# The feed-forward networks of a two-layer trunk: up products first, then the down product as seven accumulated block products

## The reference

```python
def conv_ffn(h, w_up, conv_w, conv_b, w_down):
    a = h @ w_up                                  # 256x1024 @ 1024x5632
    a = lax.conv_general_dilated(a, conv_w[:, None, :], window_strides=(1,), padding=((1, 1),),
                                 feature_group_count=2 * D_FF, ...) + conv_b
    g, u = jnp.split(a, 2, axis=-1)
    return (jax.nn.gelu(g, approximate=True) * u) @ w_down    # 256x2816 @ 2816x1024

# in each of two layers:
    h = rms_norm(x, ffn_pre_g[l])
    x = x + rms_norm(conv_ffn(h, ...), ffn_post_g[l])
```

## Time and profile before

| what | us |
|---|---|
| time, median of 3 runs (1779.08 to 1784.57) | 1782.12 |
| span of the profiled execution, first to last instruction | 1778.3 |
| TensorE busy | 1723.2 |
| VectorE busy | 812.8 |
| ScalarE busy | 412.3 |
| GpSimd busy | 76.2 |

### The profile page before, as it was taken

How to read it: one execution, slowest core, us unless ns; L and a number is a source line. 1 busy time by engine, 2 the same in 40 slices (tenths; PEclk the granted TensorE clock), 3 DMA queues, 4 the chain that set the end, 5 groups by cost and what they waited for, 6 DMA issues and landing times.

```text
span 1778.3 us, 28776 instructions
## 1 busy us (share of the span) xinstructions
PE 1723.2 (97%) x11902; PEld 1392.8 (78%) x11902; DVE 812.8 (46%) x1807; ACT 412.3 (23%) x903; POOL 76.2 (4%) x68
## 2 busy tenths in 40 slices
PE   7999999999999999999999999999999899999997
PEld 4767787666656666679788889999897688899996
DVE  4898444111111111145534445665566344576665
ACT  3743311000000000021632221111314522311112
POOL 1012001000000000010002110000000010000000
PEclk9999999999999999999999999999999999999999
DMA  9121784999999999954323244444443133244420
GB/s 396 76 71 63 294 329 178 396 422 422 422 422 422 422 421 422 422 217 144 117 95 142 95 142 157 156 165 163 146 148 139 63 127 119 95 166 166 161 77 24
DMA packets 53662, 383.50 MB, mean 216 GB/s; under 512 B 6080, under 2 KB 6336, under 8 KB 7360
## 3 DMA queue, kind: packets, MB, share of 16 engines
q1 hardware_dynamic: 52272, 376.91, 54.1%
q10 hardware_dynamic: 1296, 5.24, 0.8%
HBM read 381.08 MB, written 1.05 MB: 215 GB/s over the span
## 4 chain that ended last, share of the span: by engine, by line
PE 91%; DVE 5%; ACT 2%; DMA 1%; POOL 1%; issue 1%; POOLq 0%; ACTq 0%; DVEq 0%
PE ps L630 88%; PE ps L628 2%; DVE arena L2199 2%; PE ps L687 1%; DVE arena L2205 1%; DMA xT<-in_xc 1%; POOL arena L523 1%; DVE small L2770 0%; ACT arena L1985 0%; DVE arena L2615 0%; DVE arena L2202 0%; ACT arena L2058 0%; ACT arena L1747 0%; DVE xT L2199 0%; DVE small L2199 0%
## 5 line engine op out<-in xcount | busy, mean ns | idle before, releaser
L630 PE MATMUL ps<-arena,ring 128*128 128x256 f32 (+2 forms) x3248 | 602.5, 343 | 9.6 <-DVE arena L2199 2.1
L630 PEld LDWEIGHTS ps<-arena,ring 128*128 128x128 f32 x3248 | 507.4, 191 | 83.4 <-issue 37.6
L630 PE MATMUL ps<-ring,arena 128*64 128x256 f32 (+5 forms) x3120 | 458.1, 414 | 0.0
L630 PE MATMUL ps<-arena 128*128 128x128 f32 (+6 forms) x3178 | 416.3, 292 | 4.9 <-ACT arena L2058 1.7
L630 PEld LDWEIGHTS ps<-arena 128*128 128x128 f32 (+3 forms) x3178 | 381.9, 190 | 29.4 <-issue 14.1
L630 PEld LDWEIGHTS ps<-ring,arena 128*64 128x64 f32 (+1 forms) x3120 | 272.9, 147 | 168.1 <-issue 84.4
L2199 DVE TENSOR_TENSOR arena<-arena,ps 128x256 f32<-128x256 f32 (+2 forms) x256 | 98.5, 404 | 208.9 <-ACT arena L1955 202.8
L2205 DVE SCALAR_TENSOR_TENSOR arena<-arena,par 128x255 f32<-128x255 f32 (+1 forms) x282 | 125.7, 488 | 6.5 <-ACT arena L2175 2.3
L630 PE MATMUL ps<-ring 128*128 128x256 f32 (+2 forms) x896 | 114.4, 291 | 0.4 <-issue 0.4
L2670 DVE COPY arena<-ps 128x128 f32<-128x128 f32 x60 | 17.5, 291 | 207.4 <-PE ps L630 207.4
L630 PEld LDWEIGHTS ps<-ring 128*128 128x128 f32 (+2 forms) x896 | 97.2, 154 | 13.6 <-issue 1.9
(11 more groups left out here) (197 smaller groups left out, 1031.6 us busy)
## 6 DMA issues: line engine op xcount, KB each, us to landing
ring<-in_stream SPq DMA_DIRECT2D x358, 1024.0 KB, 9.9
arena<-in_xc ACTq DMA_DIRECT2D x1, 1024.0 KB, 6.2
xT<-in_xc ACTq DMA_DIRECT2D x1, 1024.0 KB, 10.7
arena<-in_mem ACTq DMA_DIRECT2D x1, 1024.0 KB, 4.7
out_y<-xT ACTq DMA_DIRECT2D x2, 512.0 KB, 2.6
ring<-in_dft ACTq DMA_DIRECT2D x1, 512.0 KB, 8.7
arena<-in_sguw ACTq DMA_DIRECT2D x2, 256.0 KB, 3.0
row<-in_row SPq DMA_DIRECT2D x1, 474.0 KB, 24.3
```

Source lines behind the costliest of these rows:

```text
L630: i = nc.tensor.matmul(out, lhsT, rhs, start=start, stop=stop, skip_group_check=skip)
```

## The change

The plain down slots become block products too, and the order changes. Nothing else of the computation is touched; three semaphores are folded into others, and a DMA scratch area is made smaller to give room to a tensor `extra`.

- The up slots of all pairs come first, then the eleven down slots. The stream of weights is stored in that order. All eleven gated products are kept (`f_all`).
- `down(steps)`: seven block products for each of four groups p of output chunks (banks 2p and 2p + 1), 28 products with 128 moving columns in a slot, accumulated over all slots in PSUM in all eight banks, joined once at the end (four joins into `ffn_out`). The first down slot takes the groups in the order 2, 3, 0, 1, since banks 0 to 3 still hold the last up slots; the last two slots are done together, group by group.
- `slot_sums(n)`, VectorE: weight sums of slot n, three slots ahead of TensorE (three buffers `wf` in place of two); for a down slot (n >= 20) also four sums of blocks of the gated product, on 128x128.
- VectorE per pair: join w = 0, slot sums, join w = 1, slot sums, side taps, gated product.
- `y_squares` reads the joined result instead of PSUM.

```diff
-                up_first()
-                for i in range(FFN_PAIRS):
-                    if i + 1 < FFN_PAIRS:
-                        up(i + 1)
-                    down(i)
+                up_first()
+                for i in range(1, FFN_PAIRS):
+                    up(i)
+                for i in range(FFN_PAIRS - 2):
+                    down([i])
+                down([FFN_PAIRS - 2, FFN_PAIRS - 1])
+                pe.wait_ge(cb_ok, joins_at(l, "down", 1))
...
-                def down(i):
-                    s = arrive()
-                    pe.wait_ge(f_ok, f + 1)
-                    for o in range(KC):
-                        for k in range(2):
-                            mm(bank(4 + o // 2, 2, T)[:, o % 2, :], ring[...], fT[:, i % 2, k, :], ...)
+                def down(steps):
+                    slots = [arrive() for _ in steps]
+                    order = (2, 3, 0, 1) if steps[0] == 0 else range(4)
...
+                        wt, mov = {0: (a11, f[:, 0, 0:P]), 1: (a12, f[:, 1, 0:P]), 2: (w[:, 1], fs[:, 1]),
+                                   3: (w[:, 3], f[:, 1, P:T]), 4: (a22, fs[:, 3]), 5: (w[:, 0], fs[:, 0]),
+                                   6: (w[:, 2], fs[:, 2])}[r]
+                        mm(products(2 * p)[:, r, :], wt[:, p, :], mov, i == 0 and r in (0, 4), False, ...)
...
+                    for i in steps:
+                        pe.wait_ge(f_ok, FFN_PAIRS * l + i + 1)
+                        sums_ready(i)
+                    for p in order:
+                        if steps[0] == 0 and p < 2:
+                            pe.wait_ge(cb_ok, joins_at(l, "ffn", UP_SUMS - 1 + p))
+                        for i, s in zip(steps, slots):
+                            for r in (0, 1, 4, 5, 2, 6, 3):
+                                product(i, s, r, p)
...
             def y_squares(m, y, g):
+                if m % 3 == 2:
+                    for p in range(4):
+                        act.wait_ge(cb_ok, joins_at(m // 3, "down", p + 1))
+                        A_(sq[:, 2 * p:2 * p + 2, :], ffn_out..., ACT.Square).then_inc(xq_ok, 2)
...
+                def slot_sums(n):
+                    if n >= UP_SUMS + 3:
+                        dve.wait_ge(dn_ps, down_done(l, n - UP_SUMS - 3))
+                    if n >= UP_SUMS:
+                        link(tt(to[:, 0], b12, b11, SUB))
+                        tt(to[:, 2], b22, b12, SUB)
+                        link(tt(to[:, 1], b22, to[:, 0], SUB))
+                        tt(to[:, 3], b21, to[:, 1], SUB)
+...
-                for w in range(2):
-                    weight_sums(up_slot(l, 1) + w, ws[w])
+                for n in range(3):
+                    slot_sums(n)
                 for i in range(FFN_PAIRS):
                     if i:
                         for w in range(2):
-                            dve.wait_ge(up_ps, ...)
+                            dve.wait_ge(up_ps, up_done(l, 2 * (i - 1) + w))
                             join(2 * w, ...)
-                    if more:
-                        weight_sums(up_slot(l, i + 1), ws[0])
+                            slot_sums(2 * i + 1 + w)
                     side_taps(i)
-                    if more:
-                        weight_sums(up_slot(l, i + 1) + 1, ws[1])
-                    tt(fT[:, i % 2], ...).then_inc(f_ok, 1)
+                    tt(f_all[i], ...).then_inc(f_ok, 1)
+                for n in range(UP_SUMS + 3, UP_SUMS + FFN_PAIRS):
+                    slot_sums(n)
+                for p in range(4):
+                    dve.wait_ge(y_sum, y_at(l, "ffn", p + 1))
+                    join(2 * p, halves(ffn_out[:, p, :]), halves(ffn_out[:, p + 4, :]), p % 2)
```

More of the change, by code:

```diff
@@ L335, in trunk_kernel @@
         ca = A(8704, 2, 4, T)
-        fT = A(10752, 2, 2, T)
+        f_all = [A(6656 + 512 * i, 2, T) for i in range(4)] + [A(10752 + 512 * i, 2, T) for i in range(2)] \
+            + [view(extra, 512 * i, 2, T) for i in range(5)]
+        f_sums = [view(extra, 2560 + 512 * i, 4, P) for i in range(3)]
         xg = A(8704, KC, T)
@@ L439, in up_slot, with ffn_slot, down_blocks, ffn_blocks @@
                     n += 3 * FFN_PAIRS + 2
-            return n + (3 * i - 1 if i else 0)
+            return n + 2 * i
+        def ffn_slot(l, n):
+            return up_slot(l, 1) + n
+        def down_blocks(v):
+            v = v.rearrange("p (k h q m) -> p h k q m", k=2, h=2, q=4)
+            return v[:, 0, 0], v[:, 0, 1], v[:, 1, 0], v[:, 1, 1]
+        def ffn_blocks(l, n):
+            slot = ring[:, (BASE + ffn_slot(l, n) % LATE) % SLOTS, :]
+            return (blocks if n < UP_SUMS else down_blocks)(slot)
+        def up_done(l, n):
+            return (UP_SUMS + 1) * l + n + 2 + l // (LAYERS - 1)
+        def down_done(l, i):
+            return (FFN_PAIRS - 2) * l + i + 1
         turn_bank = (1, 3, 4, 1)
@@ L1622, in _, with product, sums_ready @@
-                up_first()
-                for i in range(FFN_PAIRS):
-                    if i + 1 < FFN_PAIRS:
-                        up(i + 1)
-                    down(i)
+                def down(steps):
+                    slots = [arrive() for _ in steps]
+                    for i, s in zip(steps, slots):
+                        assert BASE + (ffn_slot(l, UP_SUMS + i)) % LATE == s
+                    tail = len(steps) > 1
+                    order = (2, 3, 0, 1) if steps[0] == 0 else range(4)
+                    def product(i, s, r, p):
+                        at = UP_SUMS + i
+                        a11, a12, a21, a22 = down_blocks(ring[:, s % SLOTS, :])
+                        f, fs, w = f_all[i], f_sums[i % 3], wf[at % 3]
+                        wt, mov = {0: (a11, f[:, 0, 0:P]), 1: (a12, f[:, 1, 0:P]), 2: (w[:, 1], fs[:, 1]),
+                                   3: (w[:, 3], f[:, 1, P:T]), 4: (a22, fs[:, 3]), 5: (w[:, 0], fs[:, 0]),
+                                   6: (w[:, 2], fs[:, 2])}[r]
+                        last = r == 3 and (tail or p == order[3])
+                        mm(products(2 * p)[:, r, :], wt[:, p, :], mov, i == 0 and r in (0, 4), False, skip=True,
+                           inc=None if not last else dn_ps if not tail else y_sum if i == steps[-1] else None)
+                    def sums_ready(i):
+                        pe.wait_ge(wsum_ok, sums_at(l, "ffn", UP_SUMS + i + 2))
+                    for i in steps:
[4 more added lines that the diff above has]
+                            pe.wait_ge(cb_ok, joins_at(l, "ffn", UP_SUMS - 1 + p))
+                        for i, s in zip(steps, slots):
+                            for r in (0, 1, 4, 5, 2, 6, 3):
+                                product(i, s, r, p)
+                    for _ in steps:
+                        release()
@@ L2945 @@
             put(np.stack([up[i], up[FFN_PAIRS + i]]))
-            if i:
-                put(down[i - 1:i])
-        put(down[FFN_PAIRS - 1:])
+        put(down)
         if l + 1 < LAYERS:
```

62 lines of the change are left out of this document (38 added, 24 removed).

## The result

| kernel | median of its runs, us | to the kernel before, on the same chip |
|---|---|---|
| before | 1781.38 (1779.08 to 1784.57, 4 runs) | |
| after | 1791.04 (1791.0 to 1793.4, 4 runs) | 1.0059 [1.0045, 1.0073] |

A forecast was written before the change was run, and what follows sets the result against it. TensorE bounds the kernel before; VectorE was to set the up stage's pace after. Terms -14.5 - 2.5 + 12.0 + 5.8 + 2.7 + 2.5 = +6.0, plus 2.8 for clock, give +8.8: 1790.9, stated as 1791; 1781 to 1798 should hold 8 in 10.

The forecast's parts named there:

- 22 down slots, 6.25 for 6.91: TensorE's down slots as block products take the up slot's 6.25 us, saving 0.66 each: -14.5 us.
- last down slot's wait gone: The last down slot no longer waits for its gated product, 1.05 plus about 0.16 in both layers: -2.5 us.
- VectorE's round in the up stage: VectorE needs 13.53 us a pair against TensorE's 12.50, making TensorE wait from slot 8: +12.0 us.
- join in the first down slot: TensorE waits 2.8 us inside each first down slot for slot 19's join, 2.9 with resuming: +5.8 us.
- third set of sums, layer 1: A third set of weight sums ahead of layer 1's first side taps lengthens TensorE's wait to 3.5: +2.7 us.
- last join: At the networks' ends a join comes between last product and squares, +1.2 and +1.3: +2.5 us.
- sum without clock: The six terms of slots, waits and joins together, before any clock drop: +6.0 us.
- clock behind the waits: Three waits longer than 2.35 us may halve TensorE's clock, 1.7 a drop; somewhat under two drops taken: +2.8 us.
- The token sums: Four 128x128 block sums of the gated product on VectorE, near the first down slot, take 1.06 us.
- the +11.1 with three drops behind the waits: The sum by the Trainium skill's clock rule alone, with drops behind all three long waits: +11.1 us.
- the rival come true: Rival: VectorE keeps up in every up-stage round, its waits and the clock term vanish: -11.8, 1770 us; chance 8%.
- Scattered products: Rival: down-slot products to changing PSUM blocks take 0.123 a record, not 0.112: +14.5 on top, 1805 us; chance 5%.

The follow-up runs named there:

- experiment 2: After with the gated products on GpSimd instead of VectorE, ScalarE waiting for them two pairs later: 1769.94 us, ratio 0.9944 to before.
- Experiment 6: After with the weight sums of slot 2i + 2 split, two operations ahead of the side taps and two behind: 1774.74 us, ratio 0.9964 to before.
- experiment 1: After with the whole set of weight sums of slot 2i + 2 moved behind the side taps: 1799.82 us, ratio 1.0115 to before.
- experiment 3: After's order and three buffers, but plain down slots as before (16 products, 256 moving columns, no sums or joins): 1794.65 us, ratio 1.0084 to before.
- experiment 7: After with both joins ahead of the two sets of sums in the last round: 1784.46 us, ratio 1.0022 to before.
- experiment 4: After with layer 1's third set of weight sums behind the side taps of pair 0: 1785.56 us, ratio 1.0032 to before.
- experiment 5: After with gated products on GpSimd and layer 1's third set of sums behind its first side taps: 1765.85 us, ratio 0.9913 to before.
- experiment 8: Before with only the folded semaphores, smaller DMA scratch and unused tensor extra: 1780.3 us, ratio 1.0 to before.
- experiment 9: Experiment 5's kernel with plain down slots (16 products, 256 moving columns, no down sums or result joins): 1777.6 us, ratio 0.9987 to before.

## Why the prediction was right, and where it was not

| step of the prediction | predicted | measured |
|---|---|---|
| 22 down slots, 6.25 for 6.91 | -14.5 | -14.3 (6.26) |
| last down slot's wait gone | -2.5 | the waits of 1.05 and 1.04 are gone, -2.1; the 0.16 each not separable |
| VectorE's round in the up stage | 13.53; +12.0 | 13.52; 5.93 + 5.83 = +11.8 (after against experiment 2) |
| join in the first down slot | +5.8 | 2.79 + 2.80 = +5.6 |
| third set of sums, layer 1 | +2.7 | 3.52 - 0.85 = +2.7 |
| last join | +2.5 | 1.21 + 1.38 = +2.6 |
| sum without clock | +6.0 | +5.8 (7.3 less 1.5) |
| clock behind the waits | +2.8 | +1.5 |
| drops of the clock elsewhere | none foreseen | +3.6 |
| span | +8.8 | +10.9 |

*The time.* That 1791 was met to a tenth is luck. The rise was forecast as 8.8 and measured as 9.7, and it was added to a median of three runs of before (1782.1) that a fourth run moved to 1781.4. What the forecast had right is the mechanism and the six terms without the clock: +6.0 for +5.8.

*The pace of the products.* Writing to changing blocks of PSUM costs nothing that shows. The 81 ns of the Trainium skill (TensorE: Matmul & The Clock Gate, Back-to-back issue gap) for sustained products with weight loads do not hold here: a record's step is 0.112 us. At two passes a record that is its other figure, 56 ns.

*The round.* It was summed from rows of single groups and of one unusual place, the last pair, which had no sums behind its side taps. That place showed the wait that the new order would put into every round, and was the best row of the trace before. The first wait came at slot 8 as worked out, and the first up stage took 130.99 us, 131.1 by the forecast's starts. Experiments 2 and 6 show the mechanism from two sides: one takes work out of the round, the other only covers its waits, and in both the up stage is back at 125.06.

*The first down slot.* The token sums took 1.06, as I had chosen. The row shows 2.53 for 2.8, but the sum went by steps and the row goes by a record's modelled end: three groups, 4.69 us, after 1208.64 are 1213.33, and TensorE starts again at 1216.02, 2.7 later. The stages say 2.8 (against experiment 2), where 2.9 was summed.

*The clock: the mis-sized term.* Three waits were over 2.35 and I priced somewhat under two drops; one came, behind 3.52, at 4.43 - 2.92 = 1.5. The step that failed is "these waits are no shorter than the one that did it": 2.53 is longer than 2.35, and no drop followed it in either layer. The +3.6 from two drops elsewhere made up for that, by luck; the +11.1 with three drops behind the waits is further off still, for 7.3 was measured. They were put at nothing, although the trace of before had a drop behind no wait, at 813.1 (see the last section). The total was closer than its clock terms were, and the waits that a change makes are not enough to forecast such drops.

*The rivals.* VectorE did not keep up: it missed by 1.02 a round, of which 0.80 is the gelu and 0.22 is work. Experiment 2 is the rival come true, and at its price: its stages and tails are 10.1 under before, 11.7 without the clock drop behind the 3.50, and -11.8 was the sum. Experiment 6 comes close to it by moving two operations. Scattered products are not slower.

## What to carry to other kernels

Before moving work out from between two dependent steps of an engine, list what it covers at either place: here one set of sums could cover ScalarE's taps or its gelu, each choice alone lost, and half at each place was enough, though the round stayed 0.22 over TensorE's. When two engines alternate, sum the round of each by starts, waits included; an engine that was idle a third of the time becomes the bound once the other's work in its round shrinks, and then a saving on TensorE is worth only what the other allows (6.1 us here, 11.8 with VectorE relieved).

## What the runs showed of the hardware

**The clock behind a wait.** Drops to 1.2 GHz came at the end of all waits of 3.50 to 3.52 (after and experiments 1, 2, 3, 6, 7) and of both of 2.82 in experiment 1. They were 3.40 us long each, but for the one of 6.8 us at experiment 1's 3.50. None came with the waits of 2.50 to 2.53 (after and experiment 4, two each), 1.28 or 0.85. One came with the wait of 2.35 in layer 1's attention in before, after and experiments 1, 3, 4, 5, 7, 8 and 9, but not in experiments 2 and 6. The length of the wait alone does not decide. Drops also came without any wait, in products with 32 moving columns. The same 56 records in before, layer 0 and layer 1, and in after, layer 1:

```profile
809.18 8.04 PE L630 MATMUL ps<-ring,arena 128*128 128x32 f32 x56
...
1313.04 6.41 PE L630 MATMUL ps<-ring,arena 128*128 128x32 f32 x56
```

```profile
1316.51 8.04 PE L657 MATMUL ps<-ring,arena 128*128 128x32 f32 x56
```

The drop at 813.1 is inside the first stretch and the one at 1320.3 inside the last, and in both TensorE was busy throughout; the middle one had no drop and took 1.6 us less. Of the layer 0 stretch, before, after and experiments 1, 4 and 6 had a drop, of the layer 1 stretch after and experiments 3, 4, 7 and 8. The Trainium skill (TensorE: Matmul & The Clock Gate, What's actually happening) ties the clock to how busy the engine has lately been; for the waits of 3.5 the traces agree, and that 2.35 can do what 2.53 does not is no contradiction to it, but no run here shows what decides between them. The drops in stretches that the profile shows as busy throughout it does not explain as it stands. Which of these drops an execution has is left open, and with it about 3.6 us of this comparison, and the part of experiment 7's gain that its stages don't show.

**GpSimd beside VectorE.** While GpSimd multiplied in experiment 2 (1147.20 to 1148.47), the pair of VectorE operations begun at 1148.14 took 1.61 in place of 1.41; the join's four at 1146.69, which read PSUM, took the 1.52 that they take alone. The Trainium skill (SBUF — State Buffer, Summary: rules for kernel authors) says that a VectorE operation with two SBUF inputs and a GpSimd operation that reads SBUF exclude each other, the second waiting for the first. The trace agrees in kind: of the 0.33 us that GpSimd's operation still had to run, 0.2 show. It cost no more a round, since the join's PSUM reads fill most of the 1.27.
